# A hybrid decoder layer: which queue stores u, where y's stores stand, and when the last two low parts of u are made

## The reference

```python
u = RMSNorm_pre(x)                      # x: 2048 tokens x 1024 channels, fp32
p = u @ W_in                            # six projections of 512 channels each, and two of 4 (the gates)
rg_x, rg_gate, ml_q, ml_k, ml_v, ml_o, ml_i, ml_f = split(p)
y_rg = RMSNorm(RG_LRU(conv4(rg_x)) * gelu(rg_gate))
y_ml = headRMSNorm(sigmoid(ml_o) * mLSTM(silu(conv4(ml_q)), silu(conv4(ml_k)), ml_v, ml_i, ml_f))
x  = x + RMSNorm_post(concat(y_rg, y_ml) @ W_out)
x  = x + RMSNorm_post(relu(RMSNorm_pre(x) @ W_up)^2 @ W_down)
```

## Time and profile before

| | |
|---|---|
| median of 3 runs | 2485.05 us (2482.65 to 2485.51) |
| profiled execution, own time | 2486.36 us |
| its span, first to last instruction | 2484.7 us |
| PE busy | 2318.3 us, 93% of the span, 10549 matmuls |
| DVE, ACT, POOL busy | 1287.4, 658.8, 799.8 us |
| mean granted clock of TensorE | 0.968 of full |
| q1 (SP), q0 (POOL) | 141.20 MB, 94.52 MB |

### The profile page before, as it was taken

The page is one execution under the profiler, slowest core; times in us unless marked ns, Lnnn a source line. Parts: engine busy times, 40 slices in busy tenths (PEclk is TensorE's granted clock), DMA queues, the critical chain, the costliest instruction groups (busy, mean ns, idle before and its releaser), DMA issues.

```text
span 2484.7 us, 29562 instructions
## 1 busy us (share of the span) xinstructions
PE 2318.3 (93%) x10549; PEld 1902.8 (77%) x10549; DVE 1287.4 (52%) x1665; ACT 658.8 (27%) x1187; POOL 799.8 (32%) x490
## 2 busy tenths in 40 slices
PE   5976789999999599999999999979899999999998
PEld 4754668888888487888888888868688888888886
DVE  5634646665756355455345435517755435544535
ACT  5542434544545332011001101104211101100112
POOL 5000100000000106556336435620646435633630
PEclk9988889999999699999999999989899999999999
DMA  5334244554552452112012111237512111101203
GB/s 188 112 129 158 75 145 155 164 169 150 182 160 80 144 186 92 53 60 59 26 50 68 40 36 59 71 114 237 161 51 68 37 39 59 56 28 51 68 17 144
DMA packets 123689, 244.82 MB, mean 99 GB/s; under 512 B 12785, under 2 KB 45905, under 8 KB 123633
## 3 DMA queue, kind: packets, MB, share of 16 engines
q1 hardware_dynamic: 95024, 141.20, 17.1%
q0 software_dynamic: 26304, 94.52, 12.3%
q10 hardware_dynamic: 2304, 8.39, 0.8%
HBM read 193.61 MB, written 50.46 MB: 98 GB/s over the span
## 4 chain that ended last, share of the span: by engine, by line
PE 60%; DVE 3%; ACT 1%; issue 1%; DMA 1%; POOL 0%; ACTq 0%; DVEq 0%; SPq 0%; PEldq 0%; POOLq 0%
PE o_ps L1356 20%; PE o_ps L1358 20%; PE o_ps L1357 20%; DVE o_relu L1632 1%; ACT o_ps L1457 1%; DVE o_ff_lo L1636 1%; PE o_ps L1380 0%; DMA o_v_lo<-ylo_d 0%; DVE o_acc L1576 0%; DVE o_v_lo L1625 0%; DMA o_w_raw<-in_w_out 0%; DVE o_h_t L1592 0%; ACT o_ff_hi L1514 0%; DVE o_h_t L1605 0%; POOL w_lo L1327 0%
## 5 line engine op out<-in xcount | busy, mean ns | idle before, releaser
L1325 POOL TENSOR_TENSOR w_hi<-o_w_raw,one 128x1024 fp32r<-128x1024 f32 x100 | 191.2, 1912 | 684.6 <-PE o_ps L1358 582.3
L1356 PE MATMUL o_ps<-o_v_hi,w_hi 128*128 128x512 f32 x1024 | 400.2, 391 | 4.8 <-DVE o_v_lo L1625 4.8
L1358 PE MATMUL o_ps<-o_v_hi,w_lo 128*128 128x512 f32 x1024 | 399.7, 390 | 0.0
L1357 PE MATMUL o_ps<-o_v_lo,w_hi 128*128 128x512 f32 x1024 | 399.7, 390 | 0.0
L1646 DVE TENSOR_TENSOR o_acc<-o_ps,o_acc 128x512 f32<-128x512 f32 x224 | 154.2, 690 | 376.9 <-PE o_ps L1358 376.4
L1632 DVE TENSOR_TENSOR o_relu<-o_relu 128x512 f32<-128x512 f32 x128 | 220.1, 1720 | 180.8 <-ACT o_relu L1511 180.1
L420 PE MATMUL m_unit_ps<-u_hi,w_hi 128*128 128x512 f32 x768 | 311.7, 406 | 0.0
L1511 ACT ACTIVATE o_relu<-o_ps 128x512 f32<-128x512 f32 x128 | 76.5, 598 | 873.3 <-PE o_ps L1358 842.0
L420 PE MATMUL m_unit_ps<-u_hi,w_lo 128*128 128x512 f32 x768 | 302.3, 394 | 0.0
L420 PE MATMUL m_unit_ps<-u_lo,w_hi 128*128 128x512 f32 x768 | 301.7, 393 | 0.0
L1636 DVE TENSOR_TENSOR o_ff_lo<-o_relu,o_ff_hi 128x512 fp32r<-128x512 f32 x128 | 243.7, 1904 | 90.8 <-ACT o_ff_hi L1514 90.8
(11 more groups left out here) (281 smaller groups left out, 3458.3 us busy)
## 6 DMA issues: line engine op xcount, KB each, us to landing
o_w_raw<-in_mlp_w_up POOLq DMA_DIRECT2D x64, 512.0 KB, 4.6
o_w_raw<-in_mlp_w_down POOLq DMA_DIRECT2D x64, 512.0 KB, 3.6
u_hi<-uhi_d SPq DMA_DIRECT2D x12, 2048.0 KB, 10.8
u_lo<-ulo_d SPq DMA_DIRECT2D x12, 2048.0 KB, 15.2
w_raw<-in_w_in POOLq DMA_DIRECT2D x24, 512.0 KB, 4.9
uhi_d<-u_hi SPq DMA_DIRECT2D x4, 2048.0 KB, 10.0
ulo_d<-u_lo SPq DMA_DIRECT2D x4, 2048.0 KB, 15.1
m_rows<-rows_d SPq DMA_DIRECT2D x16, 512.0 KB, 5.3
```

Of the source, the lines that this page charges most:

```text
L1325: pool.tensor_tensor(w_hi[i], w_raw[i % 2][:], one_bc, ALU.mult).then_inc(w_split[i], 1)
L1356: nc.tensor.matmul(dst, sh, mh, start=(i == 0), stop=False)
L1357: nc.tensor.matmul(dst, sh, ml, start=False, stop=False)
L1358: last = nc.tensor.matmul(dst, sl, mh, start=False, stop=(i == n - 1))
```

## The change

Three things, all in the first four steps; the loops behind them are the same.

- **u's stores** move from SP's queue to POOL's, and each tile's are cut into three parts (blocks 0 to 2, 3 to 5, 6 and 7 of the eight), each of two transfers (768, 768 and 512 KB) that are issued once their blocks' `ulo_made` have come.
- **SP** stores y of step p-1 around the saving of the rows of step p and ahead of the loads of rows and of u; the part of `load_rows` that saved rows becomes `save_rows`.
- **DVE** makes the last two low parts of u ahead of `rg_low` (L957) and `chunk_rows`, not behind them.

```diff
+        U_PARTS = ((0, 3), (3, 6), (6, KT))
...
-            def store_u(t):
-                sp.wait_ge(ulo_made, KT * (t + 1))
-                for dst, src in ((k["uhi_d"], u_hi), (k["ulo_d"], u_lo)):
-                    sp.dma_start(dst[:, :, t * TILE:(t + 1) * TILE], src[:, t % 2].bitcast(F32)).then_inc(u_out[t % 2], 16)
...
-            store_u(0)
-            load_rows(0)
-            store_u(1)
-            load_rows(1)
-            store_u(2)
-            store(0)
-            load_rows(2)
-            store_u(3)
-            load_u(4, 0)
-            store(1)
-            load_rows(3)
-            load_u(5, 1)
-            store(2)
-            load_rows(4)
-            store(3)
+            for p in range(NT):
+                if p:
+                    store_rg(p - 1)
+                save_rows(p)
+                if p:
+                    store_ml(p - 1)
+                load_rows(p)
+                if p >= 2:
+                    load_u(p + 2, p % 2)
+            load_rows(NT)
+            store(NT - 1)
...
+            def store_u(t, part):
+                first, last = U_PARTS[part]
+                pool.wait_ge(ulo_made, KT * t + last)
+                for dst, src in ((k["uhi_d"], u_hi), (k["ulo_d"], u_lo)):
+                    pool.dma_start(dst[:, first:last, t * TILE:(t + 1) * TILE], src[:, t % 2, first:last].bitcast(F32)
+                                 ).then_inc(u_out[t % 2], 16)
...
+            load_x(1)
+            for part in range(len(U_PARTS)):
+                store_u(0, part)
             for t in range(NT - 1):
-                load_x(t + 1)
                 gate_rows(t)
-            pool.wait_ge(x_tr, KT * NT)
+                store_u(t + 1, 0)
+                store_u(t + 1, 1)
+                if t + 2 < NT:
+                    load_x(t + 2)
+                store_u(t + 1, 2)
             for c in range(3):
                 load_raw(c, 1)
             gate_rows(NT - 1)
...
                 low_of("x")
                 if mix:
                     rg_square_sums(m)
+                low_parts_x(5)
+                if mix:
                     rg_low(m)
                 if gates:
                     chunk_rows(p)
-                low_parts_x(5)
```

More of the change, by code:

```diff
@@ L196, in build_mixers @@
         x_tr, uhi_made, ulo_made = sem("x_tr"), sem("uhi_made"), sem("ulo_made")
-        u_out = [sem(f"u_out{b}") for b in range(2)]
+        u_out = k["u_out"]
         if_mm, if_copied, gates_out, gates_in = sem("if_mm"), sem("if_copied"), k["gates_out"], k["gates_in"]
@@ L235, in load_u @@
                 if isinstance(p, int):
-                    sp.wait_ge(u_out[b], 64)
+                    sp.wait_ge(u_out[b], 64 * len(U_PARTS))
                 for dst, src in ((u_hi, "uhi_d"), (u_lo, "ulo_d")):
                     sp.dma_start(dst[:, b].bitcast(F32), k[src][:, :, ds((p % NT) * TILE, TILE)]).then_inc(u_in[b], 16)
-            def store_u(t):
-                sp.wait_ge(ulo_made, KT * (t + 1))
-                for dst, src in ((k["uhi_d"], u_hi), (k["ulo_d"], u_lo)):
-                    sp.dma_start(dst[:, :, t * TILE:(t + 1) * TILE], src[:, t % 2].bitcast(F32)).then_inc(u_out[t % 2], 16)
             def load_rows(p):
@@ L249, in load_rows @@
                 if isinstance(p, int) and p < NT:
[L250 to L254, removed]
                     sp.wait_ge(rows_out, 32 * (p + 1))
@@ L262, in load_rows, with save_rows, store_rg, store_ml @@
                              ).then_inc(rows_in, 16)
-            def store(m):
[L265 to L269, removed]
+            def save_rows(p):
+                sp.wait_ge(const_made, 8)
+                sp.wait_ge(rows_made, p + 1)
+                for n, row in enumerate((e1_row, e2_row)):
+                    dst = k["rows_d"][n].rearrange("(g c p) -> g c p", g=NG, p=P)[:, p * CPT:(p + 1) * CPT, :]
+                    sp.dma_start(dst, row[:]).then_inc(rows_out, 16)
+            def store_rg(m):
+                sp.wait_ge(s["yrg_lo"], s.ready(m))
+                sp.dma_start(k["yhi_cols"][:, ds(m * TILE, TILE)], yrg_hi[:].bitcast(F32)).then_inc(yrg_out, 16)
+                sp.dma_start(k["ylo_cols"][:, ds(m * TILE, TILE)], g_y[:].bitcast(F32)).then_inc(yrg_out, 16)
+            def store_ml(m):
+                at = NG * SEQ
+                sp.wait_ge(s["yml_lo"], s.ready(m))
+                sp.dma_start(k["yhi_cols"][:, ds(m * TILE + at, TILE)], yml_hi[:].bitcast(F32)).then_inc(yml_out, 16)
+                sp.dma_start(k["ylo_cols"][:, ds(m * TILE + at, TILE)], y_t[:].bitcast(F32)).then_inc(yml_out, 16)
+            def store(m):
+                store_rg(m)
+                store_ml(m)
             for i in range(CPT):
@@ L602, in squares @@
                     act.wait_ge(s["mm_g"], s.ready(t - 2))
-                    act.wait_ge(u_out[t % 2], 32)
+                    act.wait_ge(u_out[t % 2], 32 * len(U_PARTS))
                 for i in range(CPT):
@@ L1741, in hybrid_layer @@
             "gates_out": ctx.enter_context(nc.semaphore("gates_out")),
+            "u_out": [ctx.enter_context(nc.semaphore(f"u_out{b}")) for b in range(2)],
             "gates_in": ctx.enter_context(nc.semaphore("gates_in")),
```

## The result

The changed kernel takes **2454.97 us** (median of 4 runs, 2453.1 to 2457.66), the kernel before 2484.89 us beside it (4 runs, 2482.65 to 2485.51): ratio 0.9882, 95% interval 0.9865 to 0.9899. It is faster by 30 us, and slower than the 2440 us that I forecast by 15, at the upper end of the range that I gave (2430 to 2455). The profiled execution took 2454.21 us, its span is 2452.1 us, its mean granted clock 0.975 (before 0.968).

A forecast was written before the change was run, and what follows sets the result against it. PE was held by y's place in SP's queue behind u's stores, stalling ACT at L646. Savings 17.5 + 28.5 + 10.6 less 0.8 and 10.0 sum to 45.8 us, giving 2440 us, range 2430 to 2455.

The forecast's parts named there:

- step 2: Earlier `gate_unit` and y landing in time bring unit k to 153.2, not 170.66: 17.5 us saved.
- the first case: All terms as summed, y landing early: 2440 us, own range 2433 to 2450; chance 0.64.
- the third case: y's stores are early but land with everything else, three steps each losing up to 5 us: 2455 us; chance 0.18.
- my sign: If the forecast is right, ACT waits under 4 us at L646 in steps 2 to 4.
- the gate weights, in steps 1 to 4: At L432, PE's waits for these loads were to be 1.3, 2.1, 2.1 and 7.9 us.
- that these waits cost no clock: Behind PE's short new waits at L432, the undisturbed 11.03 and 2.95 us hold, with no slow-clock loss.
- step 1: `gate_unit` wait shrinks 0.5 us, but later rows and gate weights make a new 1.3 us wait: 0.8 us lost.
- step 4: Unit k to unit x saves 11.3 us; with the later start, 10.6 us saved.
- step 0: u's 4.19 MB on POOL's queue delays the gates' bounce and PE's transposes: 10.0 us lost, bounds 0 and 14.5.
- my weakest term: The step 0 loss of 10.0 us, since no row shows a large store on POOL's queue.
- the low parts at `gate_unit`: Making them earlier starts PE's `gate_unit` 3.4 us sooner in steps 2 and 3 and cuts step 1's wait by 0.5.
- step 3: Same gains as step 2, bringing unit k to 231.5, not 260.01: 28.5 us saved.

The follow-up runs named there:

- the fourth experiment: Kernel before, with only SP's order changed: y stored early, u still stored whole on SP's queue behind the row loads; 2435.01 us, ratio 0.9804.
- the kernel with the bounce first: Changed kernel, with tile 0's six stores of u behind the first bounce of the gates on GpSimd's queue; 2440.94 us, ratio 0.9828.
- the last two experiments: Rows saved ahead of y_rg's stores, in the changed kernel (2451.43 us) and in the one storing u's third part behind the next bounce (2439.01 us).

## Why the prediction was right and wrong

**Right: what bound the kernel, and that y would land before it is needed.** The stall at L646 and with it the two big waits at L432 and the 9.0 us at L458 are gone, and y's order alone (the fourth experiment) gives 50 us. In step 2 it landed later than I said: step 2 starts 15 us later than in my sum (152.03 against 137.1), so y was due near 158 by the first case and near 162 by the third, and ACT went on at 162.15, after a wait of 7.49 us where my sign was under 4. In steps 3 and 4 it landed as in the first case. In none did y decide. So the total is the number of the third case, 2455 us, by chance: the late transfers that cost time were the rows.

**Wrong: the gate weights, in steps 1 to 4.** The step that failed is "two stores ahead of the saved rows, 0.5 MB, put 1.3 us on that": I carried over the landing time of the rows from before, and charged only y's bytes to it. The 5 MB on POOL's queue, which I named one line below for the weights' own landing, were not charged to the rows ahead of them, whose landing SyncE waits for. The rows took 6.3, 7.8 and 5.6 us in steps 1 to 3, before 4.5, 3.2 and 2.4. The weights behind them landed 2.0 to 2.5 us after their issue in these steps, no later than before. Moving u's third part away took 2.8, 2.5 and 1.3 us off the rows; what makes up the rest of the delay in steps 2 and 3 stays open. PE's waits at the gates were to be 1.3, 2.1, 2.1 and 7.9 us; they are 2.9, 4.6, 4.2 and 9.0: 7.3 us more.

**Wrong: that these waits cost no clock.** I took 11.03 and 2.95 us as the pace behind a short wait, since the 2.24 us in step 1 of before had none behind it. In this kernel's trace the clock was low behind each wait at L447, 1.8 us more in steps 1 to 3; with 1.6 at the end of step 1 and 0.8 in step 4 (5.7 us from L447 to unit k, 4.9 before), 7.8 us. The 1.6 us are low clock too, but not shown to come from these waits, since the kernel with u's third part later has them without one. Nor does a wait of this length always cost clock: with the rows ahead of y, waits of 2.50 and 3.10 us had none behind them. So one row of a short wait without a loss was too little to put this term at nothing.

Against these 15.1 us stands 1.5 us that step 0 cost less. By terms:

| term | predicted | measured |
|---|---|---|
| step 2 | +17.5 | +13.1 |
| step 3 | +28.5 | +24.5 |
| step 4 | +10.6 | +8.7 |
| step 1 | -0.8 | -6.5 |
| step 0 | -10.0 | -8.5 |
| sum | 45.8 | 31.3 |

(Measured from PE's rows above against the earlier trace rows: step 0 by `gate_unit` of step 1, 88.46 against 79.95; step 1 by its last transposes, which end 15.0 us later than before; step 2 by its unit k, 1.9 later; step 3 by its unit k, 22.6 sooner; step 4 by unit x, 31.3 sooner.) The two errors less step 0 are 13.6 of the 14.5 us that are missing.

**Right: the price of step 0**, in mechanism and size. PE's wait is 12.3 us (10 to 14 forecast), GpSimd's for the gates 12.9 (just under the 13 to 16), so a small store works its way behind 4.19 MB in its queue, and while u was stored the slices moved 384 to 447 GB/s, where I reckoned with 410. I had called this my weakest term. Its six issues took 0.72 to 0.78 us each, not 0.5, and it did not matter. Against the kernel with the bounce first the loss is 10.4 us at this place, the forecast's 10.0; what I missed is that it grows to 14 by step 4.

**Right: the low parts at `gate_unit`**, 1.8 us of wait in each step, 3.4 less than before in steps 2 and 3. But they brought nothing: alone no difference, and within the change most likely a loss, 5.6 us by the medians. My sum gave them 6.8 us in steps 2 and 3, and 2.6 us for the rows in step 1 as a part of the -0.8. The saving is only moved to the next wait, for the gate weights; in step 1 the later rows make a wait of 2.9 us at the gates, where there is none without the edit.

**The rule that was weighed.** The runs bear out the part that speaks against this change: the same kernel on one queue and on two takes 2417.5 and 2417.6 us. The Trainium skill, DMA: Bandwidth & Descriptors, section "Issuing engines are not separate DMA queues", says that transfers of all issuing engines share the same DMA engines; the trace agrees in so far as two 8 KB stores on SyncE's queue landed 3.5 us after issue instead of 6.3, once u's third part was not ahead of them on GpSimd's. But I had weighed it for y, where in step 2 it held too and cost nothing, and it mattered for the rows.

## What to carry to other kernels

When a transfer is moved to another queue, go through the small transfers that someone waits for on every queue, and charge the moved bytes to each; here the moved stores held up two stores of 8 KB that gate a load, and in step 0 one of 16 KB. Ask first whether the load behind such a wait needs it at all: taking the gate weights out from behind the saved rows gave 27 us by the medians. And put a time that is saved against the next wait on the same engine before it is counted, as the 3.4 us at `gate_unit` were lost at the gates. A wait of 2 to 5 us at the gates may cost another 1.5 to 2.6 us of lower clock behind it, or none; one trace of one kernel doesn't tell which.

## What the runs showed of the hardware that I had not expected

- What clock followed a short wait did not go by the wait's length. Behind 1.91, 2.82, 2.92, 4.23 and 4.63 us at the gates PE took 4.7 us to unit k (the changed kernel, and the one with the weights first), where 2.95 is the pace at full clock. With the bounce first it took 4.7, 4.4 and 5.5 behind 2.20, 4.26 and 3.85. Behind 2.36, 2.50 and 3.10 us in the last two experiments it took 3.05. The granted clock was 0.89 over 165 to 180 us of the changed kernel (behind 4.63 us) and 1.00 over 161 to 176 us of the one with the rows ahead of y (behind 3.10 us).
- The same wait of 2.4 us at the norms in step 1 left the clock high with the gate weights first (eight norm matmuls in 1.02 us) and was followed by a lower one in the changed kernel (1.44 us), which had waited 2.9 us at the gates 30 us before; and by a low one (1.84 us) in the kernel with u's third part later, which had not waited there at all. The runs don't tell what it hangs on.
- The second of two 8 KB stores landed 3.2 us after the end of its issue in step 2 of before, and 6.3 and 7.8 us in steps 1 and 2 of the changed kernel, with x and a part of u just issued on the other queue. Loads of the gate weights that took 2.1 us behind the saved rows took 8.8 to 9.1 when they were issued right behind x, u and y.
